# A fused mixer on one core: five whole units instead of ten half units between the small products of a body

## The reference

```python
q, k, v, hq, hk, logf, hv, hg = mixer_inputs(rms_norm(xp, mix_pre_g[l]) @ w_in[l], pos_p, lb_all[l])
att, nk, nv = swa_prompt(q, k, v, attn_sinks[l])
ho, S_p = hgrn2_prompt(hq, hk, logf, hv)
xp = xp + rms_norm(mixer_output(att, ho, hg, hgrn_out_g[l], w_out[l]), mix_post_g[l])
```

## Time and profile before

| | |
|---|---|
| median of three runs | 2169.54 us |
| the profiled execution | 2169.21 us, span 2167.4 us |
| TensorE busy, of the span | 2068.0 us, 95% |
| VectorE | 1146.8 us, 53% |
| ScalarE | 569.6 us, 26% |
| GpSimd | 319.3 us, 15% |
| chain of the end, by engine | TensorE 88%, VectorE 7%, ScalarE 2%, issue 2%, DMA 1% |
| mean granted TensorE clock | 0.982 |
| a tile of w_in or w_out, 512 KB, issue to landing | 3.7 us (median) |

### The profile page before, as it was taken

How to read it: one execution, slowest core, us unless ns; L and a number is a source line. 1 busy time by engine, 2 the same in 40 slices (tenths; PEclk the granted TensorE clock), 3 DMA queues, 4 the chain that set the end, 5 groups by cost and what they waited for, 6 DMA issues and landing times.

```text
span 2167.4 us, 33689 instructions
## 1 busy us (share of the span) xinstructions
PE 2068.0 (95%) x13607; PEld 1994.9 (92%) x13607; DVE 1146.8 (53%) x1867; ACT 569.6 (26%) x890; POOL 319.3 (15%) x152
## 2 busy tenths in 40 slices
PE   5999999999999988999999698899999999999996
PEld 5999999999999978988888588799999999999995
DVE  3544445544554486576675356655445544455446
ACT  4112111111111142144555444411211111111112
POOL 7111011110111124111111020211101111011100
PEclk9999999999999999999999889999999999999998
DMA  3111111111111112111010244111111111111111
GB/s 120 59 49 49 39 48 48 48 48 39 48 41 56 49 72 85 42 30 30 22 29 22 71 153 150 49 49 49 48 39 48 43 53 48 39 40 47 51 37 78
DMA packets 29879, 117.46 MB, mean 54 GB/s; under 512 B 3433, under 2 KB 4337, under 8 KB 28016
## 3 DMA queue, kind: packets, MB, share of 16 engines
q1 hardware_dynamic: 29808, 116.45, 16.7%
HBM read 105.62 MB, written 10.81 MB: 54 GB/s over the span
## 4 chain that ended last, share of the span: by engine, by line
PE 88%; DVE 7%; ACT 2%; issue 2%; DMA 1%; SPq 0%; POOL 0%; DVEq 0%; ACTq 0%; POOLq 0%
PE PS L367 25%; PE PS L368 24%; PE PS L369 24%; PE PS L499 2%; PE PS L500 2%; PE PS L501 2%; PE PS L545 2%; DVE h L1451 2%; DVE resid L1396 1%; PE PS L405 1%; DVE y L1391 1%; DMA o_raw<-in_w_out 1%; ACT sm L1163 1%; PE PS L576 1%; PE PS L589 1%
## 5 line engine op out<-in xcount | busy, mean ns | idle before, releaser
L367 PE MATMUL PS<-x_hi,w_hi 128*128 128x344 f32 x2432 | 787.6, 324 | 36.8 <-DVE w_lo L1378 23.0
L368 PE MATMUL PS<-x_lo,w_hi 128*128 128x344 f32 x2432 | 781.3, 321 | 0.0
L369 PE MATMUL PS<-x_hi,w_lo 128*128 128x344 f32 x2432 | 779.9, 321 | 0.0
L367 PEld LDWEIGHTS PS<-x_hi,w_hi 128*128 128x128 f32 x2432 | 461.6, 190 | 40.9 <-issue 25.2
L368 PEld LDWEIGHTS PS<-x_lo,w_hi 128*128 128x128 f32 x2432 | 461.6, 190 | 1.5
L369 PEld LDWEIGHTS PS<-x_hi,w_lo 128*128 128x128 f32 x2432 | 461.6, 190 | 0.0
L833 POOL TENSOR_TENSOR raw<-raw,vecs 128x1024 f32<-128x1024 f32 x110 | 218.4, 1992 | 1433.4 <-DMA raw<-in_w_gu 1261.4
L1491 DVE TENSOR_TENSOR y<-y,PS 128x344 f32<-128x344 f32 x528 | 266.2, 512 | 187.4 <-PE PS L369 187.4
L367 PE MATMUL PS<-h,w_hi 128*128 128x344 f32 x1056 | 339.5, 322 | 7.0 <-DVE h L1451 6.0
L368 PE MATMUL PS<-h,w_hi 128*128 128x344 f32 x1056 | 337.6, 320 | 0.0
L369 PE MATMUL PS<-h,w_lo 128*128 128x344 f32 x1056 | 336.4, 319 | 0.0
(11 more groups left out here) (218 smaller groups left out, 1802.0 us busy)
## 6 DMA issues: line engine op xcount, KB each, us to landing
raw<-in_w_gu SPq DMA_DIRECT2D x88, 512.0 KB, 3.6
raw<-in_w_down SPq DMA_DIRECT2D x44, 512.0 KB, 3.6
raw<-in_w_in SPq DMA_DIRECT2D x22, 512.0 KB, 3.7
raw<-in_w_out SPq DMA_DIRECT2D x19, 512.0 KB, 3.7
resid<-in_x SPq DMA_DIRECT2D x3, 1376.0 KB, 9.5
stream_x<-resid SPq DMA_DIRECT2D x3, 1376.0 KB, 4.7
resid<-stream_x SPq DMA_DIRECT2D x3, 1376.0 KB, 6.9
out_y<-resid SPq DMA_DIRECT2D x3, 1376.0 KB, 4.7
```

The lines of the kernel that those rows point to most:

```text
L367: nc.tensor.matmul(PS[:, bank, :GW], wh, vh, start=(k == 0), stop=False)
L368: nc.tensor.matmul(PS[:, bank, :GW], wh, vl, start=False, stop=False)
L369: mm = nc.tensor.matmul(PS[:, bank, :GW], wl, vh, start=False, stop=(k == last))
```

## The change

TensorE: a body has five whole units instead of ten halves and five groups of small products between them. `outputs()` and `attend(1)` of a body move behind the body's last dense unit, to the head of the next body, and run there together with `level(0)`, the first masks and scores, `level(1)` and, in even bodies, `values()`. The second group is level 2, masks, scores, level 3; then level 4 and the keys; then the states and the first transposes; then the first `attend` and the second transposes. ScalarE and VectorE get a new order of the same operations. No operation is added or removed. Lines after the first dozen of the diff are two to ten higher in the changed file.

```diff
-            def body(i):
+            def body(i, ahead):
...
-                def dense(s):
+                def dense(x):
                     units = body_units(i)
-                    if s // 2 < len(units) and units[s // 2] is not None:
-                        half_unit(units[s // 2], s % 2)
+                    if x < len(units):
+                        half_unit(units[x], 0)
+                        half_unit(units[x], 1)
...
-                dense(0)
+                ahead()
                 level(0)
-                dense(1)
+                masks(0)
+                scores(0)
+                level(1)
                 if b == 0:
                     values()
...
-                masks(0)
-                level(1)
-                scores(0)
-                dense(2)
+                dense(0)
                 level(2)
-                dense(3)
+                masks(1)
+                scores(1)
+                level(3)
...
-                level(3)
+                dense(1)
+                level(4)
+                keys_by_token()
+                dense(2)
+                states()
+                probs_by_key(0)
+                dense(3)
+                attend(0)
+                probs_by_key(1)
                 dense(4)
-                masks(1)
-                level(4)
-                scores(1)
-                dense(5)
-                keys_by_token()
-                dense(6)
-                probs_by_key(0)
-                dense(7)
-                states()
-                attend(0)
-                dense(8)
-                probs_by_key(1)
-                dense(9)
-                outputs()
-                attend(1)
+
+                def end():
+                    outputs()
+                    attend(1)
+
+                return end
...
                 decay(i, 3)
-                decay(i, 4)
-                decay(i, 5)
+                exponentials(0)
...
                     head_log(0, 0, 2, 6)
+                decay(i, 4)
...
                 elif t < TPH - 1:
                     sigmoid(t + 1)
+                divide(0)
+                unit_end(0)
+                decay(i, 5)
...
-                exponentials(0)
-                unit_end(0)
+                exponentials(1)
                 if b and t < TPH - 1:
                     logs(t + 1)
-                divide(0)
+                divide(1)
                 unit_end(1)
...
-                exponentials(1)
-                unit_end(2)
                 if i == BODIES - 1:
                     act.wait_ge(S["unit_evac"], EVAC_CREDIT + U_OUT - 2)
+                    hi_attention(0)
                     silu_gates(0)
+                unit_end(2)
+                if i < BODIES - 1:
+                    first_decays(i + 1)
                 probs(0)
...
+                weights(0)
+                sub_max(0)
+                weights(1)
                 level(i, 4)
                 decayed(i, 2)
                 decayed(i, 3)
-                weights(0)
-                weights(1)
+                over(0)
                 unit_end(0)
+                weights_low(0)
+                weights(2)
+                sub_max(1)
+                weights(3)
                 decayed(i, 4)
-                sub_max(0)
-                weights(2)
-                weights_low(0)
                 if b and t < TPH - 1:
                     gates(t + 1)
+                over(1)
+                unit_end(1)
+                weights_low(1)
+                weights(4)
```

More of the change, by code:

```diff
@@ L655, in body @@
                     head_sums(0, 2, TPH, 6)
-                level(3)
-                dense(4)
-                masks(1)
-                level(4)
-                scores(1)
-                dense(5)
-                keys_by_token()
-                dense(6)
-                probs_by_key(0)
-                dense(7)
-                states()
-                attend(0)
-                dense(8)
-                probs_by_key(1)
-                dense(9)
-                outputs()
-                attend(1)
+                dense(1)
[7 more added lines that the diff above has]
+                probs_by_key(1)
+                dense(4)
+                def end():
+                    outputs()
+                    attend(1)
+                return end
             pe.wait_ge(S["mem_zero"], 1)
+            end = lambda: None
             for i in range(BODIES):
-                body(i)
+                end = body(i, end)
+            end()
             def out_units(k0, k1):
@@ L1219, in body @@
                 nc.scalar.activation(kdT[:], PS[:, 7, :], ACT.Copy).then_inc(S["kdtc_done"], 1)
-                exponentials(1)
-                unit_end(2)
                 if i == BODIES - 1:
                     act.wait_ge(S["unit_evac"], EVAC_CREDIT + U_OUT - 2)
+                    hi_attention(0)
                     silu_gates(0)
+                unit_end(2)
+                if i < BODIES - 1:
+                    first_decays(i + 1)
                 probs(0)
                 if i < BODIES - 1:
-                    first_decays(i + 1)
-                divide(1)
+                    decay(i + 1, 1)
+                unit_end(3)
                 if i < BODIES - 1:
[L1230 to L1234, removed]
+                    decay(i + 1, 2)
+                else:
                     hi_hgrn(0)
                 probs(1)
-                if i < BODIES - 1:
-                    decay(i + 1, 2)
+                unit_end(4)
                 act.wait_ge(S["o_done"], i + 1)
@@ L1244, in body @@
                                      ACT.Copy).then_inc(S["attc_done"], 1)
-                unit_end(4)
             for i in range(BODIES):
@@ L1749, in body @@
                 decayed(i, 3)
-                weights(0)
-                weights(1)
+                over(0)
                 unit_end(0)
+                weights_low(0)
+                weights(2)
+                sub_max(1)
+                weights(3)
                 decayed(i, 4)
-                sub_max(0)
-                weights(2)
-                weights_low(0)
                 if b and t < TPH - 1:
                     gates(t + 1)
+                over(1)
+                unit_end(1)
+                weights_low(1)
+                weights(4)
                 dve.wait_ge(S["dec7"], i + 1)
                 nc.vector.tensor_tensor(dd[:, 7], dd[:, 7], batch(HQ[:, t], b), ALU.mult).then_inc(S["qk7"], 1)
[L1761 to L1766, removed]
                 if after:
                     scan(i + 1)
+                    level(i + 1, 0)
+                else:
+                    head_scaled(0)
                 unit_end(2)
[L1770 to L1773, removed]
                 weights_low(2)
-                if not after:
-                    head_scaled(0)
-                    head_gated(0)
-                unit_end(3)
                 states()
                 if not after:
+                    head_gated(0)
+                    unit_end(3)
                     weights_low(3)
                     return
-                if after:
-                    decayed(i + 1, 0)
-                    level(i + 1, 2)
-                    level(i + 1, 3)
-                    decayed(i + 1, 1)
+                level(i + 1, 1)
+                decayed(i + 1, 0)
+                level(i + 1, 2)
+                unit_end(3)
                 weights_low(3)
+                level(i + 1, 3)
+                decayed(i + 1, 1)
             for i in range(BODIES):
```

## The result

The changed kernel took 2183.83 us (median of 5, 2179.53 to 2185.08) against 2168.8 for the kernel before (2168.42 to 2170.34): ratio 1.0062, interval 1.0048 to 1.0077. Forecast were 2170.3 us and a range of 2163 to 2177.5; the result lies 6 us above the range. The profiled execution took 2185.08, 15.9 more than the one of before.

A forecast was written before the change was run, and what follows sets the result against it. TensorE was taken to bound the kernel, losing time in the mixer at dense/small boundaries and in waits for probabilities and masked copy A. Gains of 16.4 us against costs of 17.55 gave +1.1, 2170.3 us; range 2163 to 2177.5.

The forecast's parts named there:

- Probabilities and the old waits for A: Mixer: TensorE's waits for transposed probabilities, 6.1 us, and for the masked copy A, 2.5 us, were to go.
- 39 boundaries, 39 x 0.2 = 7.8 us: Mixer: 39 fewer boundaries between dense and small products on TensorE, each worth 0.2 us, were to save 7.8 us.
- Body 1: Level 3 waits 5.6 us for a masked copy behind a low-half split; one clock fall as before, nothing added.
- I take 2.0 and 0.8, nearer the low end: Waits in bodies 5 and 3, with high ends of 3.9 and 1.6 us if GpSimd holds VectorE's gates.
- Bodies 4 and 7: Waits of 1.9 and 1.3 us by late copies; body 4 with an even chance of a clock fall.
- 7 x 0.12 = 0.8: All bodies from 1: level 1 waits 0.12 us each for VectorE's operands after level 0, 0.8 us in all.
- Body 0: Waits of 1.75 us for first decayed operands and 1.2 for a masked copy; even chance of a clock fall.
- Tail: Behind the last unit: a microsecond won or lost before it moves the end equally; earlier read-out worth nothing.
- The GpSimd rival: Bodies 3 and 5: GpSimd holds VectorE's gates, stalls 1.6 and 3.9 us plus clock falls, 2176.3 us; chance 0.27.
- the splits held TensorE: Rival claimed the opposite: splits in bodies 1, 4, 5 and 7 don't hold TensorE, -12 us, 2157; chance 0.12.
- the tail gave nothing back: Rival claimed the opposite: earlier read-out shortens the gap before the head sums by 4.5 us, 2165.8; chance 0.09.
- the boundary price did go down: Rival claimed the opposite: the mixer's boundary price stays, 8 us less gain; given almost no chance.

The follow-up runs named there:

- e8: e5 with three groups of small products a body put between the halves of a unit again, 23 more boundaries: 2162.55 us, ratio 0.9964.
- e11: Changed kernel with repeated, discarded dense products on TensorE, 30 ahead of level 3 in body 1 and 20 ahead of the states in body 5: 2174.31 us, ratio 1.0025.
- e3: Changed kernel with ScalarE's last decay of a body moved back ahead of the sigmoid or copy of V: 2180.11 us, ratio 1.004.
- e2: Changed kernel with body 0's first decayed operands on VectorE moved ahead of the differences of levels 2 and 3: 2182.82 us, ratio 1.0049.
- e1: Changed kernel with VectorE's low-half splits moved behind the masked copies: 2176.01 us, ratio 1.0023.
- e6: Changed kernel with the v_cache load cut into partitions 0 to 111 and 112 to 126: 2159.86 us, ratio 0.995.
- e0: The changed kernel run again, unedited: 2180.78 us, ratio 1.0042.
- e7: e5 with the v_cache load cut into partitions 0 to 111 and 112 to 126: 2141.18 us, ratio 0.9865.
- b1: Kernel before with the v_cache load cut into partitions 0 to 111 and 112 to 126: 2153.06 us, ratio 0.9926.
- e5: Changed kernel with e3's line, VectorE's low splits moved later, and a half unit at the head of body 0: 2160.82 us, ratio 0.9952.
- e9: e5 without e3's line, so GpSimd's key decay and gain run beside the gates again: 2167.6 us, ratio 0.9991.

## Why the prediction was wrong

The mechanisms were nearly all right, and the sum of them was not. Against the forecast's +1.1 the mixer gave +10.3.

- *Probabilities and the old waits for A: right.* All went, 6.1 and 2.5 us.
- *"39 boundaries, 39 x 0.2 = 7.8 us": mis-sized.* Bodies 2 and 6 gained 0.55 us each without the 0.8, that is 0.11 a boundary and some 4.3 us in all. In body 6 ten half units took 20.5 us and five whole ones take 19.7, 0.16 saved an entry. But the small groups, now side by side, take 15.6 instead of 15.4 in sum, which the forecast's 0.2 had left out. Rows behind the number, a unit's end and level 2 behind it (the pitch in the unit is 0.16):

```profile
1171.05 0.32 PE L500 MATMUL PS<-x_lo,w_hi 128*128 128x344 f32 x1
1171.20 0.32 PE L501 MATMUL PS<-x_hi,w_lo 128*128 128x344 f32 x1
1171.46 1.11 PE L547 MATMUL PS<-dd 64*128 64x64 f32 x16
```

  The way out costs 0.1 us like the way in; the half unit of 2.09 holds both. It was also among the dearest: the ten half units of body 6 took 2.00 to 2.12, and e8's boundaries at full-array transposes cost 0.07. 3.5 us short.
- *Body 1: wait right, price incomplete.* 5.6 forecast, 5.26 measured, by the very links. The chain's links add up to 17.2, not the 17.0 written, which would have made it 5.8. That there was "one clock fall as now, so nothing further for that" was wrong twice: before, the fall is there in one profile of three (38.59; 37.09 and 37.11), and the one behind the longer wait costs 1.6 to 2.0 (e11).
- *Body 5, "I take 2.0 and 0.8, nearer the low end": the step that failed.* The stated high end was 3.9; the wait is 3.51, and a fall that costs 2.5 to 2.8 follows (e11), which the forecast had only in the rival. The body was to cost 0.3 more than before and cost 5.1. e3 shows the cause: with GpSimd moved away the gates are back at 0.81 and 0.17, and the body is 5.1 shorter. The row in hand, 1.57 us for four elements beside a gain, was the nearest one, and the rule of the Trainium skill cited with it ("GPSIMD Engine Reference", section 1) agreed; "not certain" was no reason to leave it. The trace of before had more than that one row. Counted over it: 51 VectorE instructions without a PSUM operand began inside a GpSimd gain with 0.4 us or more of it to go, and all 51 ended behind it; where the same instruction also runs without GpSimd beside it, it took half as long again at the least. Of the 89 with a PSUM operand none was longer than elsewhere. Body 3's wait was 1.1 for 0.8.
- *Bodies 4 and 7: right.* Waits of 1.63 and 0.39 for 1.9, 1.04 for 1.3; body 4's clock fell in some profiles, as the even chance had it.
- *"7 x 0.12 = 0.8" for level 1: did not come.* Level 1 waits for A in body 0 alone. This error went the other way.
- *Body 0: right in the waits' size, not in their whole cause.* Waits of 1.85 and at most 0.85 for 1.75 and 1.2; e2 showed the evacuations to hold level 0 as well. The clock fell more often than at an even chance: of six profiles with this body 0, three show the lower level for 6.8 us behind the wait (the first one, e1 and e6; the body takes 35.2 to 35.4), two for 3.4 us (e3 and e11; 33.4 and 33.5), and only e0 not at all (33.0).
- *Tail: right.* 32.6 to 33.2 us from the last unit to the head sums in every version with the slow load, so a microsecond of the mixer passed to the end. Not foreseen: the rest of the kernel behind the gap tends to be longer when TensorE stood there longer, 917.8 and 918.7 us behind 1.5 and 1.7 (e6, e7; b1 has 918.1), 919.5 and 921.4 behind 14.0 and 15.2 (before), 919.7 to 923.0 behind 19.4 to 19.8 (nine profiles). It goes with the time at the lower clock in the 60 us behind the start of the head sums: 14 us in e6, e7 and b1, 16 or 17 in both profiles of before and in e5 and e11 (919.5 to 921.4), 21 or 22 in the other seven (921.9 to 923.0). At half speed the 4 us between the last two groups are worth 2 at most; what of the first profile's 3.4 is systematic stays open.

The GpSimd rival, 2176.3, was nearest: its place came, its clock fall came, and its stalls nearly (3.5 and 1.1 for 3.9 and 1.6). With boundaries at 0.11 instead of 0.2 it would have read 2179.8. The other rivals are refuted for this kernel: the splits held TensorE, the tail gave nothing back while the slow load was there, the boundary price did go down. If the forecast's terms are laid on the bodies, the mixer's 9.2 us too little are 4.7 in body 5, 2.0 in body 0 (a fall had been taken at half), 0.8 in body 1, 0.7 in body 3, 0.3 each in bodies 2 and 6, 0.2 in body 7 and nothing to speak of in body 4. The rest of the miss lies outside: 2.6 that I take as scatter and up to 3.4 behind the gap.

## What to carry to other kernels

When an order is rewritten so that the bottleneck engine meets fewer boundaries, check for every instruction what it now waits for only because that stands ahead of it on its engine: here a low split that nobody waited for yet, a decay that woke GpSimd and an uncovered head of body 0 cost 20 us and hid a gain of 10. Price a wait of TensorE with the clock fall behind it, which came here behind each wait of 3.2 us or more, and behind some between 1.3 and 2.1. And a load of 127 partitions is worth cutting in two before anything is reordered around it: it gave 17 to 21 us.

## What the hardware showed unexpectedly

- Beside a GpSimd instruction even a VectorE copy of 128x8 from SBUF to SBUF lasts until that one is over: 1.75 (changed) and 1.23 us (e9) for 0.17 alone, and a tensor_scalar 2.40 for 0.69 (e9). A tensor_tensor of 128x256 took 2.11 instead of 0.41 in e1. Not every small one is held: a reciprocal of 128x4 took its usual 0.18 beside GpSimd (e5, 944.4). What reads PSUM is not held either: adds of 128x344 (`y<-y,PS`) took 0.51 in all 40 cases of the first profile of before that began with 0.4 us or more of a gain to go.
- A wait of 1.3 to 2.1 us may or may not bring the clock down: 1.27 (yes), 1.6 (three of six), 1.80 (yes), 1.83 (one profile of three), 1.85 at the head of body 0 (five of six), 1.95 there in e2, 2.00 and 2.09 (no), 2.13 (yes, body 4 of e3). In the mixer none up to 1.14 did, and each of 3.2 and more did.
- The issue of a w_out tile, 0.36 us in e6, took SyncE 9.86 us behind the slow load in the changed kernel, and 4.87 in the one before.
